# Token factors of two RMS norms applied behind the weight products instead of in front of them

## What is computed

```
def rms_norm(x, g):
    y = x * lax.rsqrt(jnp.mean(x * x, axis=-1, keepdims=True) + EPS)
    return y * g

def second_block(x, ...):
    x = x + hybrid_mixer(rms_norm(x, norm_mix_g), ...)                  # ends in (...) @ w_mix_out
    x = x + memory_cross_attention(rms_norm(x, norm_xattn_g), ...)      # q = h @ w_q, ..., out @ w_o
    x = x + swiglu_ffn(rms_norm(x, norm_ffn_g), w_ffn_in, w_ffn_out)    # silu(h @ gate) * (h @ up) @ w_out
    return rms_norm(x, norm_final_g)
```

## Time and profile before

| | us |
|---|---|
| median of 3 runs | 2798.62 |
| lowest and highest run | 2794.9 and 2827.63 |
| the profiled execution | 2813.04 |
| its span, from the first to the last instruction | 2811.2 |

### The profile page before, as it was taken

One profiled execution on the slowest core, in us unless ns is written; L12 is line 12 of the kernel. 1 busy time (PEld: TensorE's weight loads), 2 busy tenths in 40 slices (PEclk: granted clock), 3 DMA queues, 4 the chain that ended last, 5 costly groups with the idle time before them and its releaser, 6 DMA issues.

```text
span 2811.2 us, 51084 instructions
## 1 busy us (share of the span) xinstructions
PE 2650.1 (94%) x20916; PEld 2437.3 (87%) x20916; DVE 1463.9 (52%) x2506; ACT 1234.7 (44%) x2032; POOL 114.4 (4%) x177
## 2 busy tenths in 40 slices
PE   7998999999998699999989999989989998999998
PEld 7985899999997399999979776779956986899998
DVE  3223476553524766655467888852475343433333
ACT  3335353432425734342364877752475234333321
POOL 0000000000000000000001233300000000000000
PEclk9999999999999999999999999999999999999999
DMA  6420032223331013223344655532211321223232
GB/s 181 117 75 0 31 98 90 97 95 100 103 107 60 1 61 105 90 95 115 98 164 140 200 184 190 195 105 92 90 38 65 101 98 38 76 98 97 97 105 68
DMA packets 74702, 278.34 MB, mean 99 GB/s; under 512 B 9642, under 2 KB 9674, under 8 KB 74048
## 3 DMA queue, kind: packets, MB, share of 16 engines
q1 hardware_dynamic: 60816, 217.42, 23.2%
q0 software_dynamic: 13744, 58.88, 7.2%
HBM read 267.03 MB, written 9.24 MB: 98 GB/s over the span
## 4 chain that ended last, share of the span: by engine, by line
PE 75%; DVE 14%; ACT 7%; issue 3%; DMA 1%; SPq 0%; DVEq 0%; ACTq 0%
PE acc L338 63%; PE acc L369 2%; DVE big L1618 2%; DVE res_tmp L1911 2%; PE ps L813 1%; DMA w_raw<-in_stream 1%; DVE w_lo L319 1%; PE ps L369 1%; PE acc L1467 1%; ACT L285 1%; DVE res_tmp L1905 1%; DVE big L2214 1%; PE ps L453 1%; DVE big L1276 1%; ACT res_tmp L1882 1%
## 5 line engine op out<-in xcount | busy, mean ns | idle before, releaser
L338 PE MATMUL acc<-x_split,w_hi 128*128 128x256 f32 x7968 | 1257.9, 280 | 20.3 <-DVE x_split L1363 12.0
L338 PEld LDWEIGHTS acc<-x_split,w_hi 128*128 128x128 f32 x7968 | 1076.7, 190 | 24.6 <-issue 16.8
L319 DVE TENSOR_TENSOR w_lo<-w_raw,w_hi 128x1024 fp32r<-128x1024 f32 x405 | 494.3, 1221 | 606.9 <-ACT w_hi L313 606.9
L338 PE MATMUL acc<-x_split,w_lo 128*128 128x256 f32 x3984 | 788.8, 280 | 0.0
L313 ACT ACTIVATE w_hi<-w_raw 128x1024 fp32r<-128x1024 f32 x405 | 426.3, 1054 | 581.0 <-PE acc L338 528.1
L338 PEld LDWEIGHTS acc<-x_split,w_lo 128*128 128x128 f32 x3984 | 610.1, 190 | 0.0
L338 PE MATMUL acc<-big_r,w_hi 128*128 128x256 f32 x3560 | 563.4, 281 | 7.7 <-DVE big_r L2267 3.4
L338 PEld LDWEIGHTS acc<-big_r,w_hi 128*128 128x128 f32 x3560 | 482.6, 190 | 10.3 <-issue 4.1
L338 PE MATMUL acc<-big_r,w_lo 128*128 128x256 f32 x1780 | 353.6, 280 | 0.0
L338 PEld LDWEIGHTS acc<-big_r,w_lo 128*128 128x128 f32 x1780 | 272.8, 189 | 0.0
L958 ACT ACTIVATE res_tmp<-acc,par 128x512 f32<-128x512 f32 x84 | 64.9, 772 | 150.6 <-PE acc L338 146.0
(11 more groups left out here) (301 smaller groups left out, 2677.1 us busy)
## 6 DMA issues: line engine op xcount, KB each, us to landing
w_raw<-in_stream SPq DMA_DIRECT2D x405, 512.0 KB, 3.5
res_tmp<-scratch_rows POOLq DMA_DIRECT2D x96, 320.0 KB, 5.3
big<-scratch_rows POOLq DMA_DIRECT2D x32, 320.0 KB, 5.5
scratch_bias<-res_tmp POOLq DMA_DIRECT2D x1, 2560.0 KB, 56.6
res_tmp<-in_x SPq DMA_DIRECT2D x2, 1024.0 KB, 7.6
res_tmp<-scratch_bias POOLq DMA_DIRECT2D x8, 256.0 KB, 4.4
scratch_x<-res_tmp POOLq DMA_DIRECT2D x1, 2048.0 KB, 8.0
scratch_kv<-big POOLq DMA_DIRECT2D x1, 2048.0 KB, 9.5
```

Source lines behind the costliest of these rows:

```text
L319: dve.tensor_tensor(w_lo[:, u.slot], w_raw[:, u.slot], w_hi[:, u.slot].bitcast(F32), ALU.subtract).then_inc(lo_done, 1)
L338: mm = pe.matmul(a[:, h], w, AR[:, x + k, h], start=(k == 0 and w is wh and x == hi and h.start == 0), stop=(k == total - 1 and w is wl), ...
```

## The change

The two norms in front of `xq` and `ffn_in` no longer scale the operand with the token factor. The operand that is split is the residual times its column gain alone. It is made tile by tile inside `residual_act` (high part, a new activation with the gain as its scale) and `residual_dve` (low part). `rms_pe` moves behind the first tile of `xq` and of `ffn_in`. `factors_act` makes the token factor into an SBUF slot, `RSTD`. The evictions multiply with it: in `xq` VectorE does all eight, with 0.0625 and the factor in one instruction, and ScalarE none; in `ffn_in` VectorE evicts gate and up with one multiplication each, ScalarE's Silu then works in place on the gate, and VectorE multiplies the two from SBUF. `xq`'s eight tiles are written out on all engines instead of in a loop. The final norm is as it was.

```diff
@@ -2259,7 +2259,7 @@
             for k in range(KD):
                 act.wait_ge(ev("mixed"), k + 1)
                 act.activation(AR[:, MH + k], A[:, MIX + k], ACT.Copy).then_inc(ev("m_hi"), 1)
-            residual_act(act, "mix_out", 1)
+            residual_act(act, "mix_out", 1, "xattn_g")
 
         def mix_dve(dve):
             for k in range(KD):
@@ -2267,23 +2267,39 @@
                 dve.tensor_tensor(AR[:, ML + k], A[:, MIX + k], AR[:, MH + k].bitcast(F32),
                                   ALU.subtract).then_inc(ev("m_lo"), 1)
             dve.wait_ge(ev("x_back"), 16)
-            residual_dve(dve, "mix_out", 1)
-
-        def residual_act(act, stage, c):
+            residual_dve(dve, "mix_out", 1, "xattn_g")
+
+
+        RSTD = TMP + 6
+
+        def residual_act(act, stage, c, g):
 
             for n in range(KD):
                 split_hi(act, Units(UB[stage] + n + RING))
                 evacuated(act, Tiles(TB[stage] + n))
+                act.activation(AR[:, XH + n], A[:, RES + n], ACT.Identity, bias=0.0,
+                               scale=col(g, n)).then_inc(ev("h_hi"), 1)
                 square(act, c, RES, n)
 
-        def residual_dve(dve, stage, c):
+        def residual_dve(dve, stage, c, g):
             for n in range(KD):
                 u, t = Units(UB[stage] + n), Tiles(TB[stage] + n)
                 x = A[:, RES + n]
                 tile_done(dve, u)
                 dve.tensor_tensor(x, x, acc[t.bank][:], ALU.add).then_inc(acc_free[t.bank], 1)
                 split_lo(dve, u + RING)
+                evacuated(dve, t)
+                dve.wait_ge(ev("h_hi"), nth("h_hi", KD * c + n + 1))
+                dve.scalar_tensor_tensor(AR[:, XL + n], x, col(g, n), AR[:, XH + n].bitcast(F32), ALU.mult,
+                                         ALU.subtract).then_inc(ev("h_lo"), 1)
                 add_square(dve, c, n)
+
+        def factors_act(act, c):
+            table_of_exp_and_ln(act)
+            act.wait_ge(ev("rms_sum"), nth("rms_sum", c + 1))
+            act.activation(ps[:, 2], ps[:, 2], ACT.Ln, bias=col("eps", 1), scale=1.0 / D).then_inc(ev("rms_log"), 1)
+            act.wait_ge(ev("rms_log"), nth("rms_log", c + 1))
+            act.activation(A[:, RSTD], ps[:, 2], ACT.Exp, scale=-0.5).then_inc(ev("rms_rstd"), 1)
 
 
         XQ, XK, XV, XOH, XOL, X_SOFT, X_TURN = 16, 40, 48, 24, 32, TMP, 56
@@ -2291,7 +2307,26 @@
         XD = D // X_H // P
 
         def xq_pe(pe):
-            linear_pe(pe, "xq", XH, XL, ready=("h_lo", nth("h_lo", 1 * KD)))
+            for n in range(KD):
+                product_tile(pe, Units(UB["xq"] + n), Tiles(TB["xq"] + n), XH, XL,
+                             ready=None if n else ("h_lo", nth("h_lo", 1 * KD)))
+                if n == 0:
+                    rms_pe(pe, 1)
+
+        def xq_act(act):
+            split_hi(act, Units(UB["xq"] + RING))
+            factors_act(act, 1)
+            for n in range(1, KD):
+                split_hi(act, Units(UB["xq"] + n + RING))
+
+        def xq_dve(dve):
+            dve.wait_ge(ev("rms_rstd"), nth("rms_rstd", 2))
+            for n in range(KD):
+                u, t = Units(UB["xq"] + n), Tiles(TB["xq"] + n)
+                tile_done(dve, u)
+                dve.scalar_tensor_tensor(A[:, XQ + n], acc[t.bank][:], 0.0625, A[:, RSTD], ALU.mult,
+                                         ALU.mult).then_inc(acc_free[t.bank], 1)
+                split_lo(dve, u + RING)
 
 
         def x_stat(it, k):
@@ -2378,7 +2413,7 @@
                     result(it // CH - 1, 0)
                 if it >= 9 and it % CH == 1:
                     result(it // CH - 2, 1)
-            residual_act(act, "xout", 2)
+            residual_act(act, "xout", 2, "ffn_g")
 
         def xattn_dve(dve):
             def maximum(it):
@@ -2410,7 +2445,7 @@
                     result(it // CH - 1, 0)
                 if it >= 9 and it % CH == 1:
                     result(it // CH - 2, 1)
-            residual_dve(dve, "xout", 2)
+            residual_dve(dve, "xout", 2, "ffn_g")
 
         def xout_pe(pe):
             pe.wait_ge(ev("xo_lo"), nth("xo_lo", KD))
@@ -2418,38 +2453,49 @@
 
 
         def ffn_pe(pe):
-            linear_pe(pe, "ffn_in", XH, XL, ready=("h_lo", nth("h_lo", 2 * KD)))
+            def body(i, ready=None):
+                for j in range(4):
+                    product_tile(pe, Units(UB["ffn_in"] + j, i, 4), Tiles(TB["ffn_in"] + j, i, 4), XH, XL,
+                                 ready=None if j else ready)
+                    if ready is not None and j == 0:
+                        rms_pe(pe, 2)
+            body(0, ("h_lo", nth("h_lo", 2 * KD)))
+            with pe.Fori(1, 11) as i:
+                body(i)
 
         def ffn_act(act):
             def body(i):
                 for q in range(2):
                     gate, _, _, prod = pair_work(q)
                     u, t = Units(UB["ffn_in"] + 2 * q, i, 4), Tiles(TB["ffn_in"] + 2 * q, i, 4)
-                    tile_done(act, u)
-                    act.activation(gate, acc[t.bank][:], ACT.Silu).then_inc(acc_free[t.bank], 1)
                     split_hi(act, u + RING)
+                    evacuated(act, t)
+                    act.activation(gate, gate, ACT.Silu).then_inc(ev("silu"), 1)
                     split_hi(act, u + (1 + RING))
                     act.wait_ge(ev("prod"), 44 + 2 * i + q + 1)
                     act.activation(AR.at(GH, 2 * i + q), prod, ACT.Copy).then_inc(ev("g_hi"), 1)
+            factors_act(act, 2)
             repeat(act, 11, body)
 
         def ffn_dve(dve):
             def body(i):
                 for q in range(2):
-                    gate, _, _, prod = pair_work(q)
+                    gate, up, _, prod = pair_work(q)
                     u, t = Units(UB["ffn_in"] + 2 * q, i, 4), Tiles(TB["ffn_in"] + 2 * q, i, 4)
                     n = 44 + 2 * i + q
+                    tile_done(dve, u)
+                    dve.tensor_tensor(gate, acc[t.bank][:], A[:, RSTD], ALU.mult).then_inc(acc_free[t.bank], 1)
                     split_lo(dve, u + RING)
-                    evacuated(dve, t)
                     tile_done(dve, u + 1)
-                    dve.tensor_tensor(prod, gate, acc[(t + 1).bank][:], ALU.mult).then_inc(acc_free[(t + 1).bank], 1)
+                    dve.tensor_tensor(up, acc[(t + 1).bank][:], A[:, RSTD], ALU.mult).then_inc(acc_free[(t + 1).bank], 1)
                     split_lo(dve, u + (1 + RING))
-
                     evacuated(dve, t + 1)
-                    dve.tensor_copy(small[:, q:q + 1], prod[:, 0:1]).then_inc(ev("prod"), 1)
+                    dve.wait_ge(ev("silu"), n + 1)
+                    dve.tensor_tensor(prod, gate, up, ALU.mult).then_inc(ev("prod"), 1)
                     dve.wait_ge(ev("g_hi"), n + 1)
                     dve.tensor_tensor(AR.at(GL, 2 * i + q), prod, AR.at(GH, 2 * i + q).bitcast(F32),
                                       ALU.subtract).then_inc(ev("g_lo"), 1)
+            dve.wait_ge(ev("rms_rstd"), nth("rms_rstd", 3))
             repeat(dve, 11, body)
 
 
...
-            qkv_pe, win_pe, br_attn_pe, mix_pe, lambda e: rms_pe(e, 1), xq_pe,
-            xattn_pe, xout_pe, lambda e: rms_pe(e, 2),
+            qkv_pe, win_pe, br_attn_pe, mix_pe, xq_pe,
+            xattn_pe, xout_pe,
             ffn_pe, lambda e: down_pe(e, "ffn_out"), lambda e: rms_pe(e, 3),
...
-            lambda e: rms_act(e, 1),
-            lambda e: copy_tiles_act(e, "xq", 0, 2, XQ, 0.0625),
-            xattn_act, lambda e: None,
-            lambda e: rms_act(e, 2),
+            xq_act, xattn_act,
             ffn_act, lambda e: down_act(e, "ffn_out"),
...
-            lambda e: rms_dve(e, 1, "xattn_g"),
-            lambda e: splits_dve(e, "xq", 2),
-            xattn_dve, lambda e: None,
-            lambda e: rms_dve(e, 2, "ffn_g"),
+            xq_dve, xattn_dve,
             ffn_dve, lambda e: down_dve(e, "ffn_out"),
...
-                sp.wait_ge(ev("rms_h"), 3 * KD + k + 1)
+                sp.wait_ge(ev("rms_h"), KD + k + 1)
```

## The result

| | before | changed |
|---|---|---|
| median of 16 runs each, same chip (us) | 2806.82 | 2787.04 |
| lowest and highest run | 2794.84 and 2827.63 | 2771.61 and 2803.67 |
| ratio, with its 95% interval | 1 | 0.9938 (0.9916 to 0.9960) |
| the profiled execution, its span | 2813.04, 2811.2 | 2792.41, 2790.6 |

The changed kernel is 17.4 us quicker by the ratio (11 to 24 us by its interval), against 17.1 us forecast; the two medians lie 19.8 us apart. That is within the 2% that the prediction named, and the interval leaves no doubt on the sign.

What follows compares the result with a forecast made beforehand. TensorE was taken to bound the kernel, so only its waits at two norms could give time: 8.5 + 8.4 + 0.2 = 17.1 us off the three-run median 2798.62, forecast 2781.5 us, range 2768 to 2802 us.

Steps and rivals of the forecast that it cites:

- What bounds the kernel: TensorE's waits in front of xq and ffn_in: 15.89 and 15.80 us to the first tile's copy-out, some 10 us each loss.
- What the change removes: Before xq and ffn_in: eight token-factor scalings and their wait go; last split at T+3.2 us, 1.6 us to spare.
- T: End of the residual's last matmul before each norm; the last split (T+3.2 us) and eighth block (T+4.8) count from it.
- What it moves: Products with ones go behind tile 0 of xq and ffn_in, holding TensorE 1.72 us; 2.7 us covers the factor.
- The sum: Savings of 8.5 us at the first norm, 8.4 at the second, 0.2 at xq's end: 17.1 us off.
- What it adds: Token-factor evictions: 0.2 us gained at xq's end; VectorE in ffn_in goes from 3.9 to 5.1 us a pair, costed at nothing.
- The fourth rival: In ffn_in's 22 pairs, VectorE and ScalarE bound once the hand-over passes 10.1 us; 2 us beyond gives 2826 us; chance 0.03.
- The clock's bound: Tile 0 of xq and ffn_in: clock taken at the full level, so the gain is the full 17.1 us.
- the other end: Tile 0 of xq and ffn_in at half clock: 11.3 instead of 5.7 us, twice; gain shrinks to 5.8 us.
- The first rival: Slower 0.71 us block pace carries on through xq, ffn_in, ffn_out: 15.6 us lost, net gain 1.5, 2797 us; chance 0.24.

## Why the prediction was right

**What bounds the kernel.** Right. Both waits were there to be removed, and they were worth the same with either norm alone.

**What the change removes.** Right nearly step by step. The T of the prediction is, by the row that it uses (2287.27 for T+1.15), the start of the add, here 2284.69. From there ScalarE's product ends at T+1.7 (T+1.9), the split at T+3.0 (T+3.2), and the eighth block starts at T+4.6 (T+4.8); the prediction counted TensorE's blocks from the same T, but the first one starts 0.2 us before the add. So 1.5 us were to spare (1.6). The new activation takes 0.71 us (0.77 by the nearest row), the new subtraction 0.74 (0.74).

**What it moves.** The four passes hold the stream for 1.72 us, as worked out. Counted from the first pass with ones (2289.93), which follows the last matmul of tile 0, the factor is there after 3.9 us instead of 3.6, since ScalarE's weight split begins 0.26 us into it; the eviction is done after 4.65 us (4.4 to 4.5), TensorE wants the bank after 7.2 (7.2), so 2.5 us covered it (2.7). In `ffn_in` the eviction is done after 4.1 us (4.0). The runs with the sums moved by one tile show that this cover works as the prediction had it: without it TensorE stands for 2.3 to 2.5 us.

**The sum.** 8.62 us at each norm against 8.5 and 8.4, and 0.28 against 0.2 at the end of `xq`: 17.5 against 17.1. Tile 0, which the sum took at 0.71 us a block, went at 0.68; that is 0.24 us a norm, of which 0.1 to 0.2 shows in the total.

**What it adds.** VectorE does 91.46 us in 195 us of `ffn_in`, which is 5.10 us for each pair of 10.88 us (5.1). Its cost was put at nothing, and the added instructions bear that out: 4.1 us more a pair still cost nothing. The fourth rival's point of decision (a hand-over of 10.1 us, 5.5 us above the one worked out) is some half a us too late by the 42.8 us measured, as mechanism and place it was right. One thing was missed. ScalarE's Silu and its weight splits now change tables in each round of the loop:

```profile
L313 ACT ACT_TABLE_LOAD x12 | 15.4, 1283 | 12.8 <-DMA w_raw<-in_stream 12.6
L2473 ACT ACT_TABLE_LOAD x11 | 14.1, 1283 | 0.2
```

The kernel before has the eleven of the Silu as well, but only one in front of a weight split, which is in an earlier stage. The eleven new ones cost 14.1 us of ScalarE, and since TensorE doesn't wait in `ffn_in`, none of it is on the path.

**The clock's bound.** Right as decided: 1.00 over the joint. That the other end was real is shown by the kernel with the sums behind tile 1: at its second norm 2.30 us of idle brought blocks of up to 1.28 us. "TensorE: Matmul & The Clock Gate" in the Trainium skill, section on the HAM clock gate, has the array fall back to half its clock when it idles; the trace agrees at the second norm (0.74) and shows that a like idle of 2.11 us at the first did not do it.

**The first rival.** It had the right phenomenon and the wrong rule. The two paces exist, and `ffn_in` at the longer one costs 8.3 us (249.3 against 241.0). But they weren't carried on. Over the changed kernel and the experiments the two products with ones stood at these norms twelve times without a wait in them or behind them, and the stream behind them went at 113.3 ns twelve times, though it had been at 117.8 ns before four of them. The one remark made against this rival, that the products interrupt the stream, was the one that decided. But the prediction had no reason why the pace behind them should be the short one, and here it was lucky: with one product in place of two, `xq`, `ffn_in` and `ffn_out` went at the longer pace, and the 15.5 us are what this rival had feared (15.6). The ratio of that kernel is 0.9982.

**The size of the time.** 2781.5 us was forecast and 2787.04 measured; the gain was right to 0.3 us by the ratio, to 0.4 by the waits and to 2.7 by the medians. The term that was off is the base: the forecast was set against the median of three runs, 2798.62 us, and sixteen of the kernel before gave 2806.82, 8.2 us more. The prediction saw that the three spread over 32.7 us, and set its range by that, which held.

## What to carry to other kernels

A factor per token that must be known before a product can start may be multiplied onto the product's result instead, and its making then has a whole tile of cover rather than none; read the cover from the bank that the late eviction holds, not from the first tile that needs the factor. When a step leaves a chain, ask what ran beside it: it takes the place (here 1.14 us of a product behind 1.28 us of a table load). And where single runs scatter by more than the change is worth, count the waits on the trace and settle the sign with medians of many runs.

## What was not expected of the hardware

The two paces of a stream of weight loads and matmuls of 256 columns, 113.3 and 117.8 ns at a granted clock of 1.00, are the largest source of scatter that was found in this kernel. They differ between executions in stages that no edit touches. The first up stage is the same in the changed kernel, with 2549 matmuls in the 300 us above, and in the kernel with norm 2 alone:

```profile
400.00:700.00 300.00, 300.00 (x2650) 300.00 (x2649) 162.99 (x229) 107.88 (x134) 0.00 (x0) 1.00 0.30 100
```

The profiled executions of before and after had about 9200 matmuls at the longer pace each, 41 us of their spans, the one with norm 2 alone about 1850. "TensorE: Matmul & The Clock Gate" in the Trainium skill, section "Back-to-back issue gap", gives for a width and clock one gap of a matmul by itself, and for two widths one spacing of a stream of load and matmul pairs; it has no two paces for one stream. Here the measurement decides.

What comes behind an interruption without idle was regular in part. Behind four passes with ones of 512 columns it was always the short pace (14 of 14, with the two added in the up stages), behind two passes (of 512 columns in the kernel with one product, of 256 at the memory's norm) and behind the sixteen of a layer norm's variance (L453) always the longer one, until the next interruption. That is a pattern of these traces, and with 256 columns it doesn't hold for four passes: behind those of a layer norm's sums (L445, L447) either pace came. The kernels with the loop written out show that the pattern doesn't suffice to choose the pace of a stage, and what decides at the other interruptions stays open.
